# Value products of the dilated and memory heads written turned, two heads in two column halves

## What is computed

```python
# group B: 4 dilated heads of 64; group C: 4 heads of 64 into 256 memory tokens
o_dil = merge_heads(dilated_attention(lq, lk, lvv, dil_slopes))    # softmax(q k^T * scale + bias) v
o_mem = merge_heads(memory_attention(mq, mk, mv))                  # softmax(q k^T * scale) v
mix = jnp.concatenate([o_diff, o_dil, o_mem], axis=-1)             # 512 + 256 + 256 columns
x = x + mix @ w_out[l]
x = x + moe_ffn(rms_norm(x, ffn_norm_g[l]), ...)                   # top 4 of 32 experts
return rms_norm(x, final_norm_g)
```

## Times and profile before

| | us |
|---|---|
| median of 3 runs (lowest to highest) | 1509.52 (1509.04 to 1509.85) |
| the profiled execution | 1509.5 |
| its span in the trace | 1507.4 |
| mean granted clock of TensorE in it | 0.987 |
| PE, DVE, ACT busy share of the span | 97%, 87%, 68% |

### The profile page before, as it was taken

One profiled execution on the slowest core, in us unless ns is written; L12 is line 12 of the kernel. 1 busy time (PEld: TensorE's weight loads), 2 busy tenths in 40 slices (PEclk: granted clock), 3 DMA queues, 4 the chain that ended last, 5 costly groups with the idle time before them and its releaser, 6 DMA issues.

```text
span 1507.4 us, 20922 instructions
## 1 busy us (share of the span) xinstructions
PE 1454.8 (97%) x7010; PEld 1188.6 (79%) x7010; DVE 1304.8 (87%) x1230; ACT 1018.6 (68%) x904; POOL 199.7 (13%) x148
## 2 busy tenths in 40 slices
PE   6999999889999999999999999999999999999994
PEld 5877868878888888888888888888888888888882
DVE  6258554798999999999999999999999999999998
ACT  6344344357777777777777777777777777777771
POOL 0000000030221111111111112211111111111100
PEclk9999999899999999999999999999999999999997
DMA  9411030389999999999999999999999999999994
GB/s 341 144 57 56 33 140 15 143 318 331 374 376 370 375 375 370 376 371 371 374 371 357 368 380 368 359 379 375 376 370 374 377 371 374 366 371 357 374 367 168
DMA packets 98014, 471.55 MB, mean 313 GB/s; under 512 B 12564, under 2 KB 12605, under 8 KB 63682
## 3 DMA queue, kind: packets, MB, share of 16 engines
q1 hardware_dynamic: 87682, 451.72, 77.1%
q0 software_dynamic: 10304, 19.46, 3.5%
HBM read 467.18 MB, written 21.50 MB: 324 GB/s over the span
## 4 chain that ended last, share of the span: by engine, by line
PE 91%; DVE 5%; issue 1%; ACT 1%; DMA 1%; SPq 0%; DVEq 0%; ACTq 0%
PE gu_bank L1256 17%; PE gu_bank L1258 17%; PE gu_bank L1257 17%; PE turn_bank L1256 8%; PE turn_bank L1258 8%; PE turn_bank L1257 8%; PE bank L1524 2%; PE bank L1531 2%; PE bank L1256 2%; PE gu_bank L1516 1%; PE bank L1258 1%; PE bank L1257 1%; PE bank L1445 1%; PE gu_bank L1391 1%; DVE w_lo L834 1%
## 5 line engine op out<-in xcount | busy, mean ns | idle before, releaser
L834 DVE TENSOR_TENSOR w_lo<-raw,w_hi 128x2048 fp32r<-128x2048 f32 x411 | 932.5, 2290 | 106.9 <-ACT w_hi L578 101.3
L578 ACT ACTIVATE w_hi<-raw 128x2048 fp32r<-128x2048 f32 x411 | 785.1, 1921 | 218.0 <-PE gu_bank L1258 180.8
L1256 PE MATMUL gu_bank<-w_hi,turned 128*128 128x512 f32 x1080 | 424.3, 393 | 4.7 <-ACT arena L736 4.5
L1258 PE MATMUL gu_bank<-w_hi,turned 128*128 128x512 f32 x1080 | 420.9, 390 | 0.0
L1257 PE MATMUL gu_bank<-w_lo,turned 128*128 128x512 f32 x1080 | 420.9, 390 | 0.0
L1256 PEld LDWEIGHTS gu_bank<-w_hi,turned 128*128 128x128 f32 x1080 | 203.2, 188 | 46.7 <-issue 4.9
L1258 PEld LDWEIGHTS gu_bank<-w_hi,turned 128*128 128x128 f32 x1080 | 203.0, 188 | 42.4
L1257 PEld LDWEIGHTS gu_bank<-w_lo,turned 128*128 128x128 f32 x1080 | 203.3, 188 | 40.9
L1256 PE MATMUL turn_bank<-w_hi,turned 128*128 128x512 f32 (+1 forms) x544 | 213.4, 392 | 0.0
L1258 PE MATMUL turn_bank<-w_hi,turned 128*128 128x512 f32 (+1 forms) x544 | 210.4, 387 | 0.0
L1257 PE MATMUL turn_bank<-w_lo,turned 128*128 128x512 f32 (+1 forms) x544 | 210.3, 387 | 0.0
(11 more groups left out here) (267 smaller groups left out, 1333.2 us busy)
## 6 DMA issues: line engine op xcount, KB each, us to landing
raw<-in_w_gate_up_dram SPq DMA_DIRECT2D x264, 1024.0 KB, 7.7
raw<-in_w_down_dram SPq DMA_DIRECT2D x132, 1024.0 KB, 9.6
raw<-in_w_in_dram SPq DMA_DIRECT2D x10, 1024.0 KB, 7.2
raw<-in_w_out_dram SPq DMA_DIRECT2D x4, 1024.0 KB, 5.0
raw<-expert_rows SPq DMA_DIRECT2D x4, 1024.0 KB, 6.0
raw<-in_w_mem_kv_dram SPq DMA_DIRECT2D x2, 1024.0 KB, 11.1
arena<-in_x_dram SPq DMA_DIRECT2D x1, 2048.0 KB, 12.4
arena<-in_position_tables_dram SPq DMA_DIRECT2D x1, 2048.0 KB, 17.3
```

The lines of the kernel that those rows point to most:

```text
L578: a.activation(home, raw_ap, ACT.Copy).then_inc(hi_ready, 1)
L834: v.tensor_tensor(home[1], raw_ap, home[0].bitcast(F32), ALU.subtract).then_inc(lo_ready, 1)
L1256: pe.matmul(bank, a[0], b[0], start=first, stop=False)
L1258: return pe.matmul(bank, a[1], b[0], start=False, stop=last)
```

## The change

For group B and C the operands of V change places. The values (128 keys by 64 columns) are the stationary side and the turned probabilities (128 keys by 128 queries) stream, so the sums come out as 64 columns by 128 queries; head j of the pair writes partitions 64j to 64j+63. The key blocks are the outer loop and the two heads the inner one. The result already has the form that the output projection wants, so the four `("mix", 1, qb)` tasks go. As queries are now along the free axis, the scaling by the reciprocals can't be done on the sums; `combine` scales the probabilities of both heads instead, before they are turned (two `tensor_scalar` of 128 by n). Out of PSUM, ScalarE copies the high part (`turned_high`, 128x128) and VectorE subtracts it for the low part.

```diff
     for qb in range(1, NT):
-        tasks += short[qb][:1] + [("mix", 1, qb - 1)] + short[qb][1:]
-    return tasks + [None, ("mix", 1, NT - 1)]
+        tasks += short[qb]
+    return tasks
...
-        OUT_STEPS = (19, 20, 21, 22, 24, 28, 29, 30, 32, 33, 34, 35, 39, 40, 44, 45)
+        OUT_STEPS = (19, 20, 21, 22, 24, 26, 28, 29, 30, 31, 32, 33, 36, 37, 39, 40)
...
-        EARLY_FILL = (17, 18, 21, 24, 28, 33)
+        EARLY_FILL = (17, 18, 21, 24, 28)
...
-        for n, i in enumerate((36, 37)):
+        for n, i in enumerate((34, 35)):
...
-        SPLIT_HI = {5: 10, 7: 11, 13: 12, 18: 13, 21: 14, 25: 15, 38: 16, 40: 17}
+        SPLIT_HI = {5: 10, 7: 11, 13: 12, 18: 13, 21: 14, 25: 15, 35: 16, 37: 17}
...
-        LAST_PV = STEPS - 3
-        ALL_STEPS = max(STEPS, max(DONE) + 1)
+        LAST_PV = STEPS - 1
+        ALL_STEPS = LAST_PV + 6
...
-                    uses.append(((kind, n), (7 - 2 * (n % 2)) if kind == "in" else 6 + i % 2))
+                    uses.append(((kind, n), (7 - 2 * (n % 2)) if kind == "in" else 7 if n == len(OUTS) - 1 else 6))
             if is_real(task(i - LAG_V)):
-                uses.append((("pv", real[task(i - LAG_V)]), 6 if i < FIRST_OUT else 7 - i % 2))
+                uses.append((("pv", real[task(i - LAG_V)]), 6 if i < FIRST_OUT else 7))
...
+            def turned_high(i):
+
+                t = task(i - LAG_V)
+                if is_real(t) and t[0] != "diff":
+                    r = real[t]
+                    a.wait_ge(pv_done, r + 1)
+                    a.activation(turned_part(mix_hi[1], t), psum[BANK["pv", r]][:, 0:P], ACT.Copy).then_inc(high_done, 1)
...
+                link(v.reciprocal(st[:, 6:8], st[:, 4:6]))
                 if t[0] != "diff":
-                    v.reciprocal(st[:, 6:8], st[:, 4:6]).then_inc(prob_ready, 1)
+                    for j in range(2):
+                        p = probs[:, r % 2, j, 0:n]
+                        ins = v.tensor_scalar(p, p, st[:, 6 + j:7 + j], None, ALU.mult)
+                    ins.then_inc(prob_ready, 1)
                     return
...
+                if kind != "diff":
+                    v.wait_ge(high_done, r - N_DIFF + 1)
+                    v.tensor_tensor(turned_part(mix_low[1], t), o[:, 0:P], turned_part(mix_hi[1], t).bitcast(F32),
+                                    ALU.subtract).then_inc(out_done, 1)
+                    return
...
             for i in range(ALL_STEPS):
+                if is_real(task(i - LAG_V - 1)) and task(i - LAG_V - 1)[0] != "diff":
+                    finish(task(i - LAG_V - 1))
...
+                        values = dil_v if kind == "dil" else mem_v
+                        for j in range(2):
+                            ins = pe.matmul(bank[j * DH:(j + 1) * DH, 0:P],
+                                            values[:, kb, (2 * h + j) * DH:(2 * h + j + 1) * DH], pt[:, r % 2, j, keys],
                                             start=kb == 0, stop=kb == nb - 1)
```

66 lines of the change are left out of this document (30 added, 36 removed).

## The result

The changed kernel takes 1514.21 us (median of 9 runs, 1512.27 to 1514.70), the kernel before beside it 1509.04 us (9 runs). The ratio is 1.0030 with an interval of 1.0021 to 1.0039: slower by 0.3%, about 5 us. A second set of runs of the same two kernels gave 1.0042 (1.0028 to 1.0056). The forecast was 1510.5 us in a range of 1505 to 1517.5, that is 1.0 us above the kernel before.

A forecast was written before the change was run, and what follows sets the result against it. TensorE was taken as the bound (97% of the span), the loop moving with route_top. 11.2 us lost, 8.3 gained and 1.5 less clock loss gave +1.4, taken as +1.0 on 1509.5: 1510.5 us, range 1505 to 1517.5.

The forecast's parts named there:

- the rival on VectorE and ScalarE: Attention steps: longer chains on these engines make T wait 0.3 to 0.5 us in ten steps; 1514 us, chance 0.19.
- V: Value products in attention: two heads side by side in column halves, less mode entries, gain 3.9 us.
- Turnings and two waits gone: Attention: four turnings of finished rows (1.7 us) and waits of 1.63 and 1.07 us (2.7 us) disappear.
- Item 1: Output pieces sharing bank 6: out2 and out3 wait for earlier residual adds, 1.9 us lost at out3.
- Item 2: Scaling two probability tiles before turning delays T; fills mostly hide it, 0.5 us lost at steps 24 to 26.
- Item 3: Waits at out12 (behind ScalarE's weight half 16 and turned-fill copy), out13 and route0: 2.2, 0.6 and 1.2 us lost.
- Item 4: End of attention: root and both norms now stand uncovered behind the last add, 4.8 us lost before route_top.
- The clock: Half-clock falls up to route_top, expected near 203 and at out12, cost 3.0 us instead of 4.5: 1.5 gained.
- one for one: Behind route_top: the change is worth what it moves that start; the 63 us to the loop change by at most 1.
- that the clock stays up: Attention: shorter, spread waits cause no fall to half clock; about 1506 us, chance 0.22 jointly with the cheaper tail.
- the tail is cheap: End of attention: if the rest did not wait for route_top, 4.8 us go; 1506, chance 0.22 jointly with the clock rival.
- The column halves in turn: Value products: halves run one after the other, V loses 7.7 us; +6.5, 1517 us, chance 0.17.

The follow-up runs named there:

- a_banks2: Changed kernel with output pieces and V taking turns in banks 6 and 7 as before the change, save the last two pieces: 1507.51 us, 0.9992 of the kernel before.
- b_scale: Kernel before plus two VectorE products over the short heads' probabilities (by ones) before they are turned: 1510.93 us, 1.0013 of the kernel before.
- a_tail: Changed kernel with root and first norm back ahead of out14's residual add, second norm right behind it: 1507.93 us, 0.9986 of the kernel before.
- after_again: The changed kernel, unedited, measured a second time: 1514.18 us, 1.0042 of the kernel before.
- a_tail_hi16: Changed kernel with root and first norm ahead of out14's add and ScalarE's weight half 16 copied in step 36: 1505.49 us, 0.9974 of the kernel before.
- a_hi16: Changed kernel with ScalarE's copy of weight half 16 moved from step 35 to behind the copies of step 36: 1511.00 us, 1.0013 of the kernel before.
- a_jouter: Changed kernel with the short heads' value products issued head by head, not alternating per key block: 1515.00 us, 1.0032 of the kernel before.
- b_tail: Kernel before with root and both norms moved behind the last residual add on VectorE: 1514.44 us, 1.0036 of the kernel before.
- a_best: Changed kernel with root and first norm ahead of out14's add, and turns in banks 6 and 7 from step 34 on: 1502.53 us, 0.9960 of the kernel before.
- a_best_fill: a_best plus products nobody reads in TensorE's idle places behind the last residual add: 1500.65 us, 0.9949 of the kernel before.
- b_fill: Kernel before plus products nobody reads in TensorE's idle places behind the last residual add: 1508.27 us, 0.9994 of the kernel before.

## Why the prediction was right, and where it was not

The time is in the range, and the sign of the sum was right; the time was 3.7 us too low, and the difference to before was forecast as 1.0 us and is 4.5 by the ratio. Part of being right is luck. 1514.21 us lies above the 1507 to 1513 that I gave my own sum, in the 1512 to 1516 of the rival on VectorE and ScalarE, whose mechanism is not in the trace; and the sign hung on a small remainder of large terms. By its steps:

- **V: +3.9 us of gain forecast, about 4.6 measured.** I had 0.42, 0.63, 0.85 and 1.06 us and found 0.37, 0.59, 0.81 and 1.03. For the entry I took 0.1 and it is 0.09: 0.32 us from the last fill product to V (208.63 to 208.95), against 0.23 before:

```profile
223.82 0.39 PE L1258 MATMUL bank<-turned 128*128 128x512 f32 x1
224.05 1.00 PE L1445 MATMUL bank<-arena,raw 128*128 128x64 f32 x8
```

  With that the gain is 0.02, 0.25, 0.48 and 0.71 by nb, 4.9 us over the 16, less some 0.3 (an estimate) where a full-width instruction follows. The Trainium skill, TensorEngine Tiling (Array Packing), section Key Properties, has both sides of it, the drain at a change of mode and tiles that load and multiply independently. The trace agrees: about 0.09 us a change, and halves side by side. Its section PSUM Bottleneck says that with faster TensorE the emptying of PSUM can become the limit. Here five of the listed waits (1.98, 0.98, 2.21, 0.71 and 1.30 us) are for a bank to be read, but they come from sharing one bank: with the turns in two banks 2.21 becomes 0.41 and 0.71 goes.
- **Turnings and two waits gone, 4.4 us:** held, none of the three is in the trace.
- **Item 1, the shared bank, 1.9 us:** `out2` idles 1.98 us instead of 0.78 and V of dil0q0 starts at 194.73 instead of 192.96, so 1.8. The size was right and its meaning wrong: the turns cost as much at that place (a_banks2). I had not seen that the shared bank was a condition of item 3, nor its wait of 0.98 us at 219.66 for `out6`'s add.
- **Item 2, the scaling, 0.5 us:** mis-sized. I had 1.25 and 0.65 us of T's waits; they are 1.48 and 0.89, and there is a third of 0.94 at step 29. With 1.46 before, that is 1.9 us in the profile; b_scale, on the other kernel, gave 2.0 by the ratio.
- **Item 3, the stalls, 2.2, 0.6 and 1.2 us:** 2.21, 0.71 and 1.30. The cause was named by half: either edit takes it away.
- **Item 4, the tail, 4.8 us:** `route_top` 5.36 us behind the last add's start, as said; 4.86 us back in a_tail.
- **The clock, 3.0 us for 4.5:** falls at 252.3 and 266.0, none near 204. So the place of one was wrong, and after_again shows that such a place differs between executions of one kernel. By half the lengths of the stretches, TensorE being busy in all of them, it is 3.4 us at most against 5.1 before: 1.7 less, where I had 1.5.

With measured sizes the sum at `route_top` is -4.6 - 4.4 + 1.8 + 1.0 + 1.9 + 4.2 + 4.8 - 1.7 = +3.0 us against 1.85 in the trace. The missing 1.2 are waits that before has and I did not list (0.40 at 255.16, 0.16 at 252.16 and the like), and what I can't assign. My +1.0 there was low by 0.85.

**The step that failed** is the one behind `route_top`. I wrote that the change is worth what it moves `route_top`, one for one, and that I would be wrong if the way behind it changed by over 1 us. It changed by 1.4: I had priced the clock up to `route_top` and put it at nothing behind it. The table shows with what the two parts of the way go.

- *From the loop's first product on, 0.5 of the 1.4 us.* Without half clock there it is 22.9 us (three runs, all with the added products), with 3.4 us of it 24.2 to 24.5 (five runs), and with 6.8 us 24.9 to 25.8 (six runs). By half the time that TensorE is busy in the stretch, the estimate is 1.6 us for before and 2.1 for after; the trace has 1.5 and 2.0 above 22.9.
- *Up to the loop, 0.85 of the 1.4 us.* In eleven runs this part is 53.1 to 53.2 us, whether the clock is down in the routing for 0, 6.8, 10.2 or 13.7 us. In these it is full again 15.5 us behind `route_top` at the latest. In a_tail_hi16 it is down until 16.6 us and the part is 53.7, and in after and a_hi16 until 17.2 us and the part is 54.0. The 32 turnings of line 1498 stand there. After and after_again, the same kernel, show it: they start alike, and in the first, at half clock to 300.13 us, the next row of TensorE starts at 300.90, in the second, at half clock to 297.70, at 299.73.

Line 1498 and the start of the loop after, then the start of the loop before:

```profile
294.42 6.54 PE L1498 MATMUL bank<-arena 128*128 128x128 f32 x32 [1.79 <-DVE arena L1067]
...
336.92 0.79 PE L1270 MATMUL gu_bank<-w_hi,turned 128*128 128x512 f32 x1 [4.89 <-ACT arena L746]
```

```profile
334.22 0.79 PE L1256 MATMUL gu_bank<-w_hi,turned 128*128 128x512 f32 x1 [4.48 <-ACT arena L736]
```

After_again:

```profile
294.40 5.40 PE L1498 MATMUL bank<-arena 128*128 128x128 f32 x32 [1.78 <-DVE arena L1067]
...
336.01 0.79 PE L1270 MATMUL gu_bank<-w_hi,turned 128*128 128x512 f32 x1 [4.59 <-ACT arena L746]
```

The two executions reach the second bias products 78.9 us behind `route_top` all the same, because the one that is earlier at the loop runs more of its first products at half clock (24.9 and 25.7). Why the other lengths of half clock in the routing cost nothing is not shown; I take it that VectorE's chain sets the pace there.

The tail does lengthen the half clock in the routing: without added products it is 10.2 us in all five runs with root and norms ahead of the last add, and 13.7 or 17.1 us in all six with them behind it. That it causes the longer stretch at the loop is not shown: a_tail has the long one too, and a_jouter, which keeps the new tail, the short one. What removes that one is work for TensorE in the idle place ahead of the loop.

**Open:** the spans differ by 3.2 us, the medians by 5.2 and in the second set by 5.6. The single times of after lie near 1512.5 and 1514.3; both profiled executions were of the lower ones. Each time comes with its mean granted clock: in the first set of after 0.983 to 0.985 for the four lower ones and 0.981 or 0.982 for the five upper ones. From 0.983 to 0.981 of 1512 us, counted at half clock, is an estimated 6 us more of it, worth up to 3 us where TensorE is busy. So more half clock is the likely cause of these 2 us; where it lies, no trace shows.

The rivals: that the clock stays up and that the tail is cheap were wrong in sign (1506 is faster than before). The column halves in turn are refuted by V's 0.59 us. VectorE and ScalarE as the beat gave the nearest time, 1514, by a mechanism that isn't there: T waits at three places (1.48, 0.89 and 0.94 us), not at ten.

## What to carry to other kernels

When a chain of tasks ends earlier, look at what used to run beside its last pieces: here a root and two norms lost their cover, and the order of these steps (4.9 us in a_tail, 4.8 in b_tail) outweighed all that the faster products gave (4.6). A stall often has two conditions, an order on one engine and a buffer shared on another; ask of each whether it alone would do, and try the cheaper edit. Where TensorE idles ahead of dense work, a few products that nobody reads can pay, but price them at the mark where the paths meet again, not at the stage that they sit in.

## What the runs showed that I had not expected

- Two column halves overlap without alternating instructions as long as a head has few of them: 0.59 us for nb = 2 in either order, 1.51 instead of 1.03 for nb = 4.
- Two executions of one kernel can have their falls of the clock at other places: at 188.5 and not at 252.3, or the other way round, with the same end (277.50 and 277.54). Between a_best and a_best_fill, the same up to there, `route_top` differs by 2.0 us, 1.4 of them with such a fall. A profile of one execution can be off by that much against another before any edit has done anything.
- A profiled execution need not be a typical one. That of b_fill, with 17.1 us of half clock ahead of an edit that begins later, took 1509.3 us at a mean granted clock of 0.988; its twelve times start at 1505.7 us with 0.993.
- The same half clock is free at one place and dear 2 us further on: up to 15.5 us behind `route_top` it cost nothing in eleven runs, down until 17.2 us it cost 0.85 us in two.
